# Ten of eleven SwiGLU product blocks turned by VectorE in 32x32 squares and carried by sixteen small DMAs instead of being turned by TensorE

## The chip, the cores and the metric

One core of one Trainium2 chip. The metric is the device time of one execution in microseconds (us). The core has a matrix engine (TensorE, PE in the profile, its weight loads PEld), a vector engine (VectorE, DVE), an activation engine (ScalarE, ACT), GpSimd (POOL), a queue engine (SyncE, SP) and 16 DMA engines that serve the DMA queues of SP, ACT and POOL together.

## What is computed

One layer of a streaming encoder on x of 256 tokens x 2048 channels in fp32: a SwiGLU FFN, a gated mixer (pooling and SSD branches), a cross-attention into 256 memory tokens, and a second FFN. The change touches the two FFNs only:

```python
def swiglu(u, w1, w3, w2):
    return (jax.nn.silu(u @ w1) * (u @ w3)) @ w2

f = swiglu(rms_norm(h, ffn1_pre_g[i]), ffn1_w1[i], ffn1_w3[i], ffn1_w2[i])
h = h + 0.5 * rms_norm(f, ffn1_post_g[i])
```

w1 and w3 are 2048 x 5632, w2 is 5632 x 2048. The product silu(u @ w1) * (u @ w3) comes out with tokens on the partitions, and the multiplication by w2 wants it with the 5632 hidden features on the partitions. Somebody has to transpose it.

## The kernel before

**Tiling.** Every weight matrix is streamed in chunks: 256 rows x 512 columns, 512 KB, laid in SBUF as 128 partitions x 2 x 512. A ring of four slots (`RING`) holds a chunk three times: `raw` as loaded, `wh` its fp32r high part, `wl` the rest. A job is 8 chunks (`CD`) for w1 or w3 and 22 (`CF`) for w2. A chunk of a token-major job is 12 matmuls: 2 halves of the rows, 2 blocks of 128 tokens (`T`), and 3 products each (lines 530 to 532: wh with the low part of the activations, wh with the high part, wl with the high part).

**The four engines of a chunk.** SP loads chunk c into its ring slot when VectorE has split chunk c-4 (semaphore `low`, lines 355 to 360). ScalarE copies `raw` to `wh` (line 879) when the load has landed and TensorE has done chunk c-4 (`used`), so it runs three chunks ahead (`AHEAD`). VectorE then writes `wl = raw - wh` (line 1293). TensorE waits for `high` and `low` of the chunk (lines 509 and 510). ScalarE and VectorE keep their order by hand: `advance()` makes the next split, `to(n)` advances until chunk n is the next of TensorE, and other work is written between such calls.

**An FFN.** It has 11 pairs of jobs (`NP`), one for each block of 512 hidden columns: "gate" (w1, 8 chunks), then "up" (w3, 8 chunks). Pair 0 is written out, pairs 1 to 10 are a loop on each engine. After a gate job ScalarE writes `silu_g` (line 975). After an up job VectorE writes the product `hid` (line 1433), two instructions of 128x512, one for each 128 tokens; their last one also frees the accumulator of the up job.

**The turn.** While the next pair runs, `hid` is transposed. TensorE does it behind the third gate chunk: `turn_hidden` (line 628) waits for `hid` and for the free PSUM area, and `turn` makes 8 transposes of 128x128 (line 565) into that area. ScalarE writes the high part `hidh` from it (`hidden_high`, line 981), VectorE the rest `hidl` (`hidden_low`, line 1421), both behind `to(c0 + 3)`, c0 being the first chunk of the pair. The block of the last pair is turned behind the loop (line 638). Then 4 "down" jobs of 22 chunks multiply `hidh` and `hidl` by w2.

Of the kernel before, what the change touches and what calls it, by code (L numbers as in the profile page):

```python
# [19 lines left out]
ALU = mybir.AluOpType  # L20
# [21 lines left out]
def hybrid_block(nc, x, mem, ffn1_pre_g, ffn1_w1, ffn1_w3, ffn1_w2, ffn1_post_g, mix_pre_g, w_in, b_gate,  # L42
# [74 lines left out]
    def slot(name):  # L117
        return jobs[name][0] % 2

    def moved(name):  # L120

        return jobs[name][0] // 2 + 1
# [8 lines left out]
    areas = {0: [], 1: []}  # L131
    for q in range(4):
        areas[q % 2].append(("pre0", q))
    areas[0] += [("hidden", 0, j) for j in range(NP)]
    for q in range(4):
        areas[q % 2].append(("pre1", q))
    areas[1] += ["dt", "cs", "csT", ("cb", 0), ("cb", 1), ("cb", 2), ("cb", 3)] + [("Y", g) for g in range(GROUPS)]
# [6 lines left out]
    areas[1] += ["score1", "probT1"]  # L144
    for q in range(4):
        areas[q % 2].append(("pre3", q))
    areas[0] += [("hidden", 1, j) for j in range(NP)]

    def use(k, name):

# [10 lines left out]
    with ExitStack() as ctx:  # L161

        def at(name, kb, shape, dt=F32):
            return nc.alloc_sbuf_tensor_at(name, shape, dt, offset=BASE + int(kb * KB))
# [9 lines left out]
        hidl = at("hidl", 140, [P, DFF // P, S], F32R)  # L174
        silu_g = at("silu_g", 184, [P, T, NCOL])
        hid = at("hid", 188, [P, T, NCOL])
        F = at("F", 184, [P, T, D])

        mixh = at("mixh", 96, [P, KD, S], F32R)
# [85 lines left out]
        def sem(name):  # L265
            return ctx.enter_context(nc.semaphore(name))
# [19 lines left out]
        job_squares = sem("job_squares")  # L286
        res_ready = sem("res_ready")
        res_squares = sem("res_squares")
        var_ready = sem("var_ready")
        root_ready = sem("root_ready")  # L290
        normed = sem("normed")
# [37 lines left out]

        def lin(static, i, per):  # L330
            return static if i is None else i * per + static

        def panel(w, k, col):

# [168 lines left out]
        def _(pe):  # L503
# [51 lines left out]
            def claim_area(k, name, i=None, per=1):  # L555
                n = use(k, name) - 1
                if n >= 1:
                    pe.wait_ge(t_moved[k], lin(n, i, per))
# [46 lines left out]
                tr.then_inc(cols_ready, 1)  # L605

            def ffn(f):
                def turn_hidden(j, i=None):

                    pe.wait_ge(evacuated[slot(("up", f, 0))], lin(moved(("up", f, j)), i, 1))  # L610
                    claim_area(0, ("hidden", f, j), i)
                    turn(0, hid)

                def pair(i=None):
                    chunk[0] = first(("gate", f, 0))
                    claim(("gate", f, 0), i)
                    n = {0: 0, 1: 3}[f]
                    if i is None and f == 1:
                        turn_res(n, (0, 1))
                    before = pre_wait(n) if i is None else None  # L620
                    token_chunks(("gate", f, 0), uh, ul, range(0, 2), CD - 1, i, 2 * CD, before)
                    if i is None:
                        turn_res(n, (2, 3))
                        if f == 0:
                            turn_rows()
                    token_chunks(("gate", f, 0), uh, ul, range(2, 3), CD - 1, i, 2 * CD, before)
                    if i is not None:
                        turn_hidden(0, i - 1)
                    token_chunks(("gate", f, 0), uh, ul, range(3, CD), CD - 1, i, 2 * CD, before)
                    if i is None and f == 0:  # L630
                        pe.wait_ge(cols_ready, 4)
                    claim(("up", f, 0), i)
                    token_chunks(("up", f, 0), uh, ul, range(CD), CD - 1, i, 2 * CD)

                pair()
                with pe.Fori(1, NP) as j:
                    pair(j)
                turn_hidden(NP - 1)

                with pe.Fori(0, NJ // 2) as i:  # L640
                    chunk[0] = first(("down", f, 0))
                    for o in range(2):
                        claim(("down", f, o), i)
                        token_chunks(("down", f, o), hidh, hidl, range(CF - 2), CF - 1, i, 2 * CF)
                        pe.wait_ge(t_moved[0], use(0, ("hidden", f, NP - 1)))
                        token_chunks(("down", f, o), hidh, hidl, range(CF - 2, CF), CF - 1, i, 2 * CF)
                chunk[0] = end(("down", f, NJ - 1))
# [217 lines left out]
        def _(act):  # L865
# [99 lines left out]
            def ffn(f):  # L965
                def silu(i=None):
                    done(i, 2 * CD)
                    if i is not None:

                        act.wait_ge(evacuated[slot(("up", f, 0))], lin(moved(("up", f, 0)), i - 1, 1))  # L970
                    if i is None:

                        act.wait_ge(normed, {0: 1, 1: 2 * T + 2}[f])
                    for t in range(T):
                        a = nc.scalar.activation(silu_g[:, t], tok(slot(("gate", f, 0)))[:, t], ACT.Silu, scale=sr_ffn[:, t:t + 1])
                    a.then_inc(evacuated[slot(("gate", f, 0))], 1)

                def hidden_high(i=None, j=0):
                    act.wait_ge(t_ready[0], lin(use(0, ("hidden", f, j)), i, 1))
                    dst = hidh[:, j * M:(j + 1) * M] if i is None else hidh[:, bass.ds(i * M, M)]  # L980
                    nc.scalar.activation(dst, area(0), ACT.Copy).then_inc(t_high[0], 1)

                c0 = first(("gate", f, 0))

                def pair(i=None):
                    if i is not None:
                        at_chunk[0] = c0
                    to(c0 + 3, i, 2 * CD)
                    if i is not None:
                        hidden_high(i - 1)  # L990
                    to(c0 + CD, i, 2 * CD)
                    silu(i)
                    to(c0 + 2 * CD, i, 2 * CD)

                pair()
                with act.Fori(1, NP) as j:
                    pair(j)
                at_chunk[0] = first(("down", f, 0))
                hidden_high(None, NP - 1)
                fetch_root(1 + f)  # L1000
                d0 = first(("down", f, 0))

                if f == 0:
                    with act.Fori(0, NJ // 2) as i:
                        at_chunk[0] = d0
                        for o in range(2):
                            to(d0 + (o + 1) * CF, i, 2 * CF)
                            done(i, 2 * CF)

                            before = names[number(("down", f, o)) - 1]  # L1010
                            act.wait_ge(evacuated[slot(before)], i + moved(before))
# [262 lines left out]
        def _(dve):  # L1274
# [139 lines left out]
            def ffn(f):  # L1414
                c0 = first(("gate", f, 0))
                g, u = ("gate", f, 0), ("up", f, 0)

                def hidden_low(i=None, j=0):
                    dve.wait_ge(t_high[0], lin(high_use(0, ("hidden", f, j)), i, 1))
                    sl = slice(j * M, (j + 1) * M) if i is None else bass.ds(i * M, M)  # L1420
                    nc.vector.tensor_tensor(hidl[:, sl], area(0), hidh[:, sl].bitcast(F32), ALU.subtract).then_inc(t_moved[0], 1)

                def pair(i=None):
                    if i is not None:
                        at_chunk[0] = c0
                    to(c0 + 3, i, 2 * CD)
                    if i is not None:
                        hidden_low(i - 1)
                    to(c0 + 2 * CD, i, 2 * CD)
                    done(i, 2 * CD)  # L1430
                    dve.wait_ge(evacuated[slot(g)], lin(moved(g), i, 1))
                    for t in range(T):
                        h = nc.vector.scalar_tensor_tensor(out=hid[:, t], in0=tok(slot(u))[:, t], scalar=sr_ffn[:, t:t + 1],
                                                           in1=silu_g[:, t], op0=ALU.mult, op1=ALU.mult)
                    h.then_inc(evacuated[slot(u)], 1)

                pair()
                with dve.Fori(1, NP) as j:
                    pair(j)
                at_chunk[0] = first(("down", f, 0))  # L1440
                hidden_low(None, NP - 1)
                d0 = first(("down", f, 0))
                if f == 0:
                    with dve.Fori(0, NJ // 2) as i:
# [399 lines left out]
```

## Time and profile before

| | |
|---|---|
| median of 3 runs | 2801.12 us (2796.75 to 2801.47) |
| profiled execution: span from the first to the last instruction | 2798.7 us |
| TensorE matmuls busy | 2755.3 us, 98% of the span |
| VectorE busy | 1569.6 us, 56% |
| ScalarE busy | 1296.0 us, 46% |
| DMA, mean | 187 GB/s |
| mean granted TensorE clock | 0.994 |

The span leaves out what lies ahead of the first and behind the last instruction; it is 2.4 us below the median of the runs, and inside their spread. A matmul row shows the modelled duration of one matmul, and these overlap: what TensorE needs for a piece of work is read from the distance between the starts of rows, not from the durations. On the rows of a timeline the bracket at the end is the engine's idle time before the row and who ended it. A row "SPq" or "ACTq" is the time that the engine's sequencer took to issue a DMA, not the transfer. A wait of a DMA queue costs nothing as long as the data is there when ScalarE wants it.

### The profile page before, as it was taken

How to read it: one execution, taken by the hardware profiler on the slowest of the kernel's cores; microseconds unless marked ns; L12 is line 12 of the kernel's file. 1: busy time of each engine (PE TensorE's matmuls, PEld its weight loads, DVE VectorE, ACT ScalarE, POOL GpSimd, SP SyncE). 2: the span in 40 equal slices, each digit the busy share in tenths (PEclk: the TensorE clock that was granted, in tenths of full speed). 3: DMA queues.
4: the chain of work that ended last, by engine and by line, in shares of the span. 5: the costliest groups of instructions: out<-in, count | busy, mean ns of one | idle time of the engine just before them, and what ended most of it. 6: DMA issues, size and time to landing. Idle time of an engine off the chain costs nothing.

```text
span 2798.7 us, 39709 instructions
## 1 busy us (share of the span) xinstructions
PE 2755.3 (98%) x14332; PEld 2371.3 (85%) x14332; DVE 1569.6 (56%) x1758; ACT 1296.0 (46%) x1430; POOL 35.3 (1%) x59
## 2 busy tenths in 40 slices
PE   8999999999899999999999999999999999999998
PEld 7888888888799888989999888888978888888886
DVE  5454544444466555787787664556565544454444
ACT  5444444444354444355565554445554444444443
POOL 0000000000000000000000000000000000000000
PEclk9999999999999999999999999999999999999999
DMA  7666666666556666565665675566456666666664
GB/s 224 188 187 193 188 189 190 192 197 196 150 167 195 190 202 188 174 185 176 180 187 179 176 201 189 188 230 191 145 172 188 188 188 193 188 187 194 196 197 150
DMA packets 268277, 522.92 MB, mean 187 GB/s; under 512 B 18496, under 2 KB 18880, under 8 KB 267936
## 3 DMA queue, kind: packets, MB, share of 16 engines
q1 hardware_dynamic: 263104, 504.07, 59.7%
q0 software_dynamic: 5056, 17.68, 2.2%
q8 instruction: 57, 0.93, 0.1%
q14 instruction: 28, 0.23, 0.0%
q10 hardware_dynamic: 32, 0.01, 0.0%
HBM read 519.53 MB, written 2.16 MB: 186 GB/s over the span
## 4 chain that ended last, share of the span: by engine, by line
PE 96%; DVE 2%; DMA 0%; ACT 0%; issue 0%; DVEq 0%; SPq 0%; ACTq 0%
PE J L530 26%; PE J L532 26%; PE J L531 26%; PE J L548 5%; PE J L551 5%; PE J L550 5%; PE A L565 1%; PE A L576 1%; PE A L768 1%; PE A L767 1%; PE A L766 0%; DVE res L1341 0%; DVE wl L1293 0%; DMA raw<-in_w_in_dram 0%; PE A L757 0%
## 5 line engine op out<-in xcount | busy, mean ns | idle before, releaser
L1293 DVE TENSOR_TENSOR wl<-raw,wh 128x1024 fp32r<-128x1024 f32 x950 | 1159.2, 1225 | 1017.3 <-ACT wh L879 1010.2
L879 ACT ACTIVATE wh<-raw 128x1024 fp32r<-128x1024 f32 x950 | 1004.6, 1060 | 1241.9 <-PE J L532 1000.4
L530 PE MATMUL J<-wh,ul 128*128 128x512 f32 x2048 | 804.0, 393 | 5.8 <-DVE bT L1513 2.5
L532 PE MATMUL J<-wl,uh 128*128 128x512 f32 x2048 | 800.4, 391 | 0.0
L531 PE MATMUL J<-wh,uh 128*128 128x512 f32 x2048 | 800.2, 391 | 0.0
L530 PEld LDWEIGHTS J<-wh,ul 128*128 128x128 f32 x2048 | 386.3, 189 | 85.9 <-issue 4.3
L532 PEld LDWEIGHTS J<-wl,uh 128*128 128x128 f32 x2048 | 386.0, 188 | 80.4
L531 PEld LDWEIGHTS J<-wh,uh 128*128 128x128 f32 x2048 | 386.1, 189 | 78.5
L548 PE MATMUL J<-ul,wh 128*128 128x256 f32 x1088 | 310.4, 285 | 1.1 <-DVE wl L1293 1.1
L551 PE MATMUL J<-uh,wl 128*128 128x256 f32 x1088 | 308.4, 284 | 0.0
L550 PE MATMUL J<-uh,wh 128*128 128x256 f32 x1088 | 308.4, 283 | 0.0
L530 PE MATMUL J<-wh,hidl 128*128 128x512 f32 x704 | 274.4, 390 | 0.0
L532 PE MATMUL J<-wl,hidh 128*128 128x512 f32 x704 | 274.3, 390 | 0.0
L531 PE MATMUL J<-wh,hidh 128*128 128x512 f32 x704 | 274.2, 390 | 0.0
L548 PEld LDWEIGHTS J<-ul,wh 128*128 128x128 f32 x1088 | 209.1, 192 | 1.4 <-ACT wh L879 1.3
L550 PEld LDWEIGHTS J<-uh,wh 128*128 128x128 f32 x1088 | 209.1, 192 | 0.0
L551 PEld LDWEIGHTS J<-uh,wl 128*128 128x128 f32 x1088 | 209.0, 192 | 0.0
L531 PEld LDWEIGHTS J<-wh,hidh 128*128 128x128 f32 x704 | 132.2, 188 | 27.3
L530 PEld LDWEIGHTS J<-wh,hidl 128*128 128x128 f32 x704 | 132.2, 188 | 27.3
L532 PEld LDWEIGHTS J<-wl,hidh 128*128 128x128 f32 x704 | 132.2, 188 | 27.3
L530 PE MATMUL J<-wh,ynl 128*128 128x512 f32 x256 | 100.0, 391 | 0.0
L532 PE MATMUL J<-wl,ynh 128*128 128x512 f32 x256 | 99.8, 390 | 0.0
(239 smaller groups left out, 1895.8 us busy)
## 6 DMA issues: line engine op xcount, KB each, us to landing
raw<-in_ffn_w_dram SPq DMA_DIRECT2D x528, 512.0 KB, 4.4
raw<-in_w_in_dram SPq DMA_DIRECT2D x257, 512.0 KB, 3.8
raw<-in_w_ssd_out_dram SPq DMA_DIRECT2D x64, 512.0 KB, 4.1
raw<-in_w_pool_out_dram SPq DMA_DIRECT2D x32, 512.0 KB, 4.2
raw<-in_w_mix_out_dram SPq DMA_DIRECT2D x32, 512.0 KB, 4.5
csb<-cs_dram POOLq DMA_DIRECT2D x16, 512.0 KB, 7.4
raw<-in_pool_w_dram SPq DMA_DIRECT2D x8, 512.0 KB, 4.3
raw<-in_w_k_dram SPq DMA_DIRECT2D x8, 512.0 KB, 4.0
```

The source lines that it names most:

```text
L530: nc.tensor.matmul(o[:, t], b, wh[:, r, kk], start=(k == 0 and kk == 0), stop=False)
L531: nc.tensor.matmul(o[:, t], a, wh[:, r, kk], start=False, stop=False)
L532: mm = nc.tensor.matmul(o[:, t], a, wl[:, r, kk], start=False, stop=(k == last_k and kk == CK - 1))
L548: nc.tensor.matmul(o[:, m], h, b, start=(k == 0 and kk == 0 and m % 2 == 0), stop=False, skip_group_check=True)
L550: nc.tensor.matmul(o[:, m], h, a, start=False, stop=False, skip_group_check=True)
L551: mm = nc.tensor.matmul(o[:, m], l, a, start=False, stop=(k == last_k and kk == CK - 1), skip_group_check=True)
L565: tr = nc.tensor.transpose(o[:, m, t * P:(t + 1) * P], src[:, t, m * P:(m + 1) * P], ident[:])
L576: mm = nc.tensor.matmul(area(q % 2)[:, m, t * P:(t + 1) * P], res[:, t, c], diag[:, t], start=True, stop=True, skip_group_check=True)
L767: nc.tensor.matmul(A[:, 1, 1, c], E[:, h, P:2 * P], Xdt[:, 0, c], start=True, stop=False)
L768: mm = nc.tensor.matmul(A[:, 1, 1, c], E[:, h, 2 * P:3 * P], Xdt[:, 1, c], start=False, stop=True)
L879: nc.scalar.activation(wh[:, r], raw[:, r], ACT.Copy).then_inc(high, 1)
L1293: nc.vector.tensor_tensor(wl[:, r], raw[:, r], wh[:, r].bitcast(F32), ALU.subtract).then_inc(low, 1)
```

## The change

For the blocks of pairs 0 to 9 TensorE makes no transposes. Behind the `hid` of a pair VectorE transposes it in 32x32 squares into a new tile `turned` (`turn_blocks`, two instructions of 128x512, no cross-partition movement beyond 32 partitions). In the next pair ScalarE's queue issues, behind one split, sixteen DMAs (`move_turned`) from `turned` to a new tile `hraw`, each from 32 partitions to 32 partitions with 4 runs of 64 numbers (256 B) per partition: 32 KB each, 512 KB together. `hidh` and `hidl` are made from `hraw` in SBUF by two instructions each instead of one from PSUM, and behind `to(c0 + 6)` instead of `to(c0 + 3)`. The block of pair 10 is still turned by TensorE. Before the down jobs TensorE waits for `hid_low`.

```diff
@@ TensorE
-                    token_chunks(("gate", f, 0), uh, ul, range(2, 3), CD - 1, i, 2 * CD, before)
-                    if i is not None:
-                        turn_hidden(0, i - 1)
-                    token_chunks(("gate", f, 0), uh, ul, range(3, CD), CD - 1, i, 2 * CD, before)
+                    token_chunks(("gate", f, 0), uh, ul, range(2, CD), CD - 1, i, 2 * CD, before)
...
-                turn_hidden(NP - 1)
+                turn_hidden()
+
+                pe.wait_ge(hid_low, turned_before(f + 1))
@@ ScalarE
-                def hidden_high(i=None, j=0):
-                    act.wait_ge(t_ready[0], lin(use(0, ("hidden", f, j)), i, 1))
-                    dst = hidh[:, j * M:(j + 1) * M] if i is None else hidh[:, bass.ds(i * M, M)]
-                    nc.scalar.activation(dst, area(0), ACT.Copy).then_inc(t_high[0], 1)
+                def move_turned(i):
+
+                    act.wait_ge(turned_ready, lin(turned_before(f) + 1, i, 1))
+                    for c in range(M):
+                        for a in range(P // 32):
+                            act.dma_start(hraw[32 * c:32 * (c + 1), :, a * 64:(a + 1) * 64],
+                                          turned[32 * a:32 * (a + 1), c::4].rearrange("p b t n -> p b (t n)")).then_inc(hid_loaded, 16)
+
+                def hidden_high(i):
+                    act.wait_ge(hid_loaded, lin(16 * 16 * (turned_before(f) + 1), i, 16 * 16))
+                    for t in range(T):
+                        a = nc.scalar.activation(in_blocks(hidh[:, bass.ds(i * M, M), t * P:(t + 1) * P]), hraw_blocks(t), ACT.Copy)
+                    a.then_inc(hid_high, 1)
...
-                    to(c0 + 3, i, 2 * CD)
+                    if i is not None:
+                        to(c0 + 1, i, 2 * CD)
+                        move_turned(i - 1)
+                    to(c0 + 6, i, 2 * CD)
                     if i is not None:
                         hidden_high(i - 1)
@@ VectorE
+                def turn_blocks(i=None):
+
+                    dve.wait_ge(evacuated[slot(u)], lin(moved(u), i, 1))
+                    for t in range(T):
+                        tr = nc.vector.transpose(turned[:, :, t], hid[:, t].rearrange("p (b n) -> p b n", n=32))
+                    tr.then_inc(turned_ready, 1)
+
+                def hidden_low(i):
+                    dve.wait_ge(hid_high, lin(turned_before(f) + 1, i, 1))
+                    for t in range(T):
+                        h, l = (in_blocks(x[:, bass.ds(i * M, M), t * P:(t + 1) * P]) for x in (hidh, hidl))
+                        o = nc.vector.tensor_tensor(l, hraw_blocks(t), h.bitcast(F32), ALU.subtract)
+                    o.then_inc(hid_low, 1)
...
-                    to(c0 + 3, i, 2 * CD)
+                    to(c0 + 6, i, 2 * CD)
                     if i is not None:
                         hidden_low(i - 1)
...
                 pair()
-                with dve.Fori(1, NP) as j:
+                turn_blocks()
+                with dve.Fori(1, NP - 1) as j:
                     pair(j)
+                    turn_blocks(j)
+                pair(NP - 1)
```

On ScalarE's queue the head of the loop over the pairs stood like this before; `wh<-raw` is the split of a weight chunk:

```order
L996 ISA
L878 REGISTER_ALU
L879 ACTIVATE wh<-raw 128x1024
L875 REGISTER_ALU
L878 REGISTER_ALU
L879 ACTIVATE wh<-raw 128x1024
L878 REGISTER_ALU
L879 ACTIVATE wh<-raw 128x1024
L979 REGISTER_ALU
L981 ISA
L981 ACTIVATE hidh<-A 128x1024
```

and stands like this now:

```order
L1028 ISA
L894 REGISTER_ALU
L895 ACTIVATE wh<-raw 128x1024
L999 DMA hraw<-turned 32x4x64 x16
L891 REGISTER_ALU
L894 REGISTER_ALU
L895 ACTIVATE wh<-raw 128x1024
L894 REGISTER_ALU
L895 ACTIVATE wh<-raw 128x1024
```

The sixteen DMA issues stand between the first and the second split of a pair; the high part of the product moved behind the sixth split.

On VectorE's queue the end of pair 0 and the head of the loop stood like this before:

```order
L1433 SCALAR_TENSOR_TENSOR hid<-J,stat,silu_g 128x512 x2
L1438 UNCONDITIONAL_BRANCH
L1438 ISA
L1293 TENSOR_TENSOR wl<-raw,wh 128x1024
L1292 REGISTER_ALU
L1293 TENSOR_TENSOR wl<-raw,wh 128x1024
```

and stands like this now:

```order
L1479 SCALAR_TENSOR_TENSOR hid<-J,stat,silu_g 128x512 x2
L1454 STREAM_TRANSPOSE turned<-hid 128x16x32 x2
L1485 UNCONDITIONAL_BRANCH
L1485 ISA
L1325 TENSOR_TENSOR wl<-raw,wh 128x1024
L1324 REGISTER_ALU
L1325 TENSOR_TENSOR wl<-raw,wh 128x1024
```

The two transposes stand behind the product and ahead of the first split of the next pair.

## Rows read from the trace of the kernel before

**Rows 1.** The page: engines' busy time, and the chain that ended last.

```profile
PE 2755.3 (98%) x14332; PEld 2371.3 (85%) x14332; DVE 1569.6 (56%) x1758; ACT 1296.0 (46%) x1430; POOL 35.3 (1%) x59
...
PE 96%; DVE 2%; DMA 0%; ACT 0%; issue 0%; DVEq 0%; SPq 0%; ACTq 0%
```

**Rows 2.** Windows: 44 us of an FFN's pairs; last three columns clock, DMA share, GB/s.

```profile
150.00:194.00 44.00, 44.00 (x200) 36.56 (x199) 21.65 (x20) 18.64 (x20) 0.00 (x0) 1.00 0.66 190
```

**Rows 3.** Timeline around one turn: start us, us, engine, line, operation.

```profile
157.11 0.39 PE L532 MATMUL J<-wl,uh 128*128 128x512 f32 x1
...
157.34 1.03 PE L565 MATMUL A<-ident,hid 128*128 128x128 f32 x8
...
158.13 0.48 PE L530 MATMUL J<-wh,ul 128*128 128x512 f32 x1
...
158.45 0.40 PE L531 MATMUL J<-wh,uh 128*128 128x512 f32 x1
...
158.68 0.39 PE L532 MATMUL J<-wl,uh 128*128 128x512 f32 x1
```

**Rows 4.** Timeline of ScalarE over one pair.

```profile
149.38 1.06 ACT L879 ACTIVATE wh<-raw 128x1024 fp32r<-128x1024 f32 x1 [1.66 <-PE J L532]
152.10 1.06 ACT L879 ACTIVATE wh<-raw 128x1024 fp32r<-128x1024 f32 x1 [1.66 <-PE J L532]
154.82 1.06 ACT L879 ACTIVATE wh<-raw 128x1024 fp32r<-128x1024 f32 x1 [1.66 <-PE J L532]
158.52 1.03 ACT L981 ACTIVATE hidh<-A 128x1024 f32 x1 [2.65 <-PE A L565]
```

**Rows 5.** Timeline at the start of that pair, TensorE's first matmul and VectorE.

```profile
149.18 0.39 PE L530 MATMUL J<-wh,ul 128*128 128x512 f32 x1
...
149.47 1.41 DVE L1433 SCALAR_TENSOR_TENSOR hid<-J,stat,silu_g 128x512 f32<-128x512 f32 x2 [0.49 <-PE J L532]
150.79 1.21 DVE L1293 TENSOR_TENSOR wl<-raw,wh 128x1024 fp32r<-128x1024 f32 x1
```

**Rows 6.** Groups by line: busy us, mean ns of one, idle before and who ended it.

```profile
L1433 DVE SCALAR_TENSOR_TENSOR hid<-J,stat,silu_g 128x512 f32<-128x512 f32 x44 | 31.0, 747 | 10.5 <-PE J L532 10.5
L1641 DVE TENSOR_SCALAR yb<-yb,stat 128x512 f32<-128x512 f32 x16 | 7.1, 484 | 0.3
...
L975 ACT ACTIVATE silu_g<-J,stat 128x512 f32<-128x512 f32 x44 | 27.9, 684 | 34.3 <-PE J L532 34.3
```

**Rows 7.** DMA issues of the queues by line: ns min/median/max, first and last start.

```profile
L360 SPq DMA_DIRECT2D raw<-in_ffn_w_dram x528: 367/373/695, 1.8 to 2768.2; - x176
...
L439 SPq DMA_DIRECT2D out_dram<-res x4: 332/348/366, 2791.8 to 2795.4; - x4
...
L867 ACTq DMA_DIRECT2D rows<-in_ffn_pre_g_dram x1: 430/430/430, 0.9 to 0.9; - x1
```

**Rows 8.** Timeline of SP: issues with no wait between them.

```profile
0.88 0.40 SPq L346 DMA_DIRECT2D ident<-in_identity_dram  x1
1.33 0.43 SPq L372 DMA_DIRECT2D res<-in_x_dram  x1
1.81 0.46 SPq L360 DMA_DIRECT2D raw<-in_ffn_w_dram  x1
...
18.77 0.37 SPq L360 DMA_DIRECT2D raw<-in_ffn_w_dram  x1
19.18 0.47 SPq L377 DMA_DIRECT2D tri<-in_causal_dram  x1
19.69 0.43 SPq L378 DMA_DIRECT2D d_bc<-in_d_skip_dram  x1
```

**Rows 9.** The dt weights, 512 KB in 2048 packets of 256 B: issue, and the DMA then.

```profile
L360 SPq DMA_DIRECT2D raw<-in_w_in_dram x1: 1343/1343/1343, 779.8 to 779.8; - x1
...
DMA to landing us min/median/max: 5.3/5.3/5.3
...
DMA packets 1749, 0.51 MB, mean 255 GB/s; under 512 B 1712, under 2 KB 1712, under 8 KB 1749
```

**Rows 10.** DMAs with KB each and median us to landing, and the range of SP's loads.

```profile
raw<-in_ffn_w_dram SPq DMA_DIRECT2D x528, 512.0 KB, 4.4
csb<-cs_dram POOLq DMA_DIRECT2D x16, 512.0 KB, 7.4
...
DMA to landing us min/median/max: 3.5/4.3/11.0
```

**Rows 11.** Timeline of one split: ScalarE's high part, then VectorE's low part.

```profile
119.46 1.06 ACT L879 ACTIVATE wh<-raw 128x1024 fp32r<-128x1024 f32 x1 [1.66 <-PE J L532]
...
120.55 1.23 DVE L1293 TENSOR_TENSOR wl<-raw,wh 128x1024 fp32r<-128x1024 f32 x1 [1.49 <-ACT wh L879]
```

More of the change, by code:

```diff
@@ L133, in hybrid_block @@
         areas[q % 2].append(("pre0", q))
-    areas[0] += [("hidden", 0, j) for j in range(NP)]
+    areas[0] += [("hidden", 0, NP - 1)]
     for q in range(4):
@@ L146, in hybrid_block @@
         areas[q % 2].append(("pre3", q))
-    areas[0] += [("hidden", 1, j) for j in range(NP)]
+    areas[0] += [("hidden", 1, NP - 1)]
     def use(k, name):
@@ L176, in hybrid_block @@
         hid = at("hid", 188, [P, T, NCOL])
+        turned = at("turned", 192, [P, NCOL // 32, T, 32])
+        hraw = at("hraw", 196, [P, M, S])
         F = at("F", 184, [P, T, D])
@@ L288, in hybrid_block @@
         res_squares = sem("res_squares")
+        turned_ready = sem("turned_ready")
+        hid_loaded = sem("hid_loaded")
+        hid_high = sem("hid_high")
+        hid_low = sem("hid_low")
         var_ready = sem("var_ready")
@@ L331, in lin, with turned_before, in_blocks, hraw_blocks @@
             return static if i is None else i * per + static
+        def turned_before(f):
+            return f * (NP - 1)
+        def in_blocks(x):
+            return x.rearrange("p k (a n) -> p k a n", n=32)
+        def hraw_blocks(t):
+            return hraw[:].rearrange("p k (a t n) -> p k t a n", t=T, n=32)[:, :, t]
         def panel(w, k, col):
@@ L607, in ffn, with turn_hidden @@
             def ffn(f):
-                def turn_hidden(j, i=None):
-                    pe.wait_ge(evacuated[slot(("up", f, 0))], lin(moved(("up", f, j)), i, 1))
-                    claim_area(0, ("hidden", f, j), i)
+                def turn_hidden():
+                    pe.wait_ge(evacuated[slot(("up", f, 0))], moved(("up", f, NP - 1)))
+                    claim_area(0, ("hidden", f, NP - 1))
                     turn(0, hid)
@@ L976, in silu, with last_high @@
                     a.then_inc(evacuated[slot(("gate", f, 0))], 1)
-                def hidden_high(i=None, j=0):
-                    act.wait_ge(t_ready[0], lin(use(0, ("hidden", f, j)), i, 1))
-                    dst = hidh[:, j * M:(j + 1) * M] if i is None else hidh[:, bass.ds(i * M, M)]
-                    nc.scalar.activation(dst, area(0), ACT.Copy).then_inc(t_high[0], 1)
+                def move_turned(i):
[9 more added lines that the diff above has]
+                    a.then_inc(hid_high, 1)
+                def last_high():
+                    act.wait_ge(t_ready[0], use(0, ("hidden", f, NP - 1)))
+                    nc.scalar.activation(hidh[:, (NP - 1) * M:NP * M], area(0), ACT.Copy).then_inc(t_high[0], 1)
                 c0 = first(("gate", f, 0))
@@ L998, in ffn @@
                 at_chunk[0] = first(("down", f, 0))
-                hidden_high(None, NP - 1)
+                last_high()
                 fetch_root(1 + f)
@@ L1416, in ffn, with last_low @@
                 g, u = ("gate", f, 0), ("up", f, 0)
-                def hidden_low(i=None, j=0):
-                    dve.wait_ge(t_high[0], lin(high_use(0, ("hidden", f, j)), i, 1))
-                    sl = slice(j * M, (j + 1) * M) if i is None else bass.ds(i * M, M)
+                def turn_blocks(i=None):
[9 more added lines that the diff above has]
+                    o.then_inc(hid_low, 1)
+                def last_low():
+                    dve.wait_ge(t_high[0], high_use(0, ("hidden", f, NP - 1)))
+                    sl = slice((NP - 1) * M, NP * M)
                     nc.vector.tensor_tensor(hidl[:, sl], area(0), hidh[:, sl].bitcast(F32), ALU.subtract).then_inc(t_moved[0], 1)
@@ L1437, in ffn @@
                 pair()
-                with dve.Fori(1, NP) as j:
+                turn_blocks()
+                with dve.Fori(1, NP - 1) as j:
                     pair(j)
+                    turn_blocks(j)
+                pair(NP - 1)
                 at_chunk[0] = first(("down", f, 0))
-                hidden_low(None, NP - 1)
+                last_low()
                 d0 = first(("down", f, 0))
```

## The prediction

> **What bounds the kernel now.** I read the page first: TensorE is busy 98% of the span, and the chain that ended last lies to 96% on it [rows 1]. The next question is whether it is short of anything in the pairs of the FFNs, where the change is. The window of 44 us there shows TensorE busy for all 44.00 us at full clock, VectorE for 21.65 and ScalarE for 18.64, the DMA engines two thirds busy at 190 GB/s [rows 2]. So in a pair the time is the number of matmuls and nothing else, and work taken from TensorE is time gained, as long as the other engines still deliver each chunk by its turn. The timeline shows how close that is. ScalarE starts a split every 2.72 us (149.38, 152.10, 154.82) and has idled 1.66 us before each, waiting for TensorE [rows 4]; 2.72 us is the pace of a chunk. It runs three chunks ahead, so it can be late by some chunks once, but not without limit.
>
> **What is removed.** The turn: the 8 transposes start at 157.34, the next matmul at 158.13, 0.79 us later, and the one behind that 0.32 us later (158.45) where 0.23 is usual (158.68) [rows 3]. That is 0.79 + 0.09 = 0.88 us. It happens in 10 pairs of 2 FFNs: 20 x 0.88 = **17.6 us**, all on TensorE's path. The PSUM area's handoffs (ScalarE's 1.03 us from PSUM [rows 4]) go from a place where nobody waits for them to another such place.
>
> **What is added, on VectorE.** Two transposes per pair, 128x512 in fp32, SBUF to SBUF. The trace has none. An instruction of that size with one input from SBUF takes 484 ns, the one with two inputs, one of them in PSUM, 747 ns [rows 6]; I take 0.6 us, nearer to the one-input row, so 1.2 us for two (ends: 1.0 and 1.5). The first split of the pair on VectorE is that much later, and it has almost three chunks of room, so by itself this costs nothing; it counts only as the start of what follows. The two-part `hidl` costs some 0.2 us more than before in VectorE's idle half: nothing.
>
> **What is added, on ScalarE's queue.** This is the term that decides. Let S be the first matmul of a pair, 149.18 in the trace [rows 5]. VectorE begins the product at S + 0.29 and has both halves at S + 1.70 (149.47 + 1.41 = 150.88) [rows 5]. With 0.05 for the semaphore and 1.2 for the transposes, `turned` is there at S + 2.95, and ScalarE, which has made one split (149.38 to 150.44, [rows 4]), passes its wait at about S + 3.0. Then its sequencer issues 16 DMAs, and behind them, on the same in-order queue, stands the split of the pair's fifth chunk (the second split of the pair; before, it started at 152.10 = S + 2.92). That split takes 1.06 us, VectorE starts 0.03 later and takes 1.23 [rows 11]; with 0.05 to reach TensorE this is 2.37 us. TensorE wants this chunk after four chunks, at S + 4 x 2.72 = S + 10.88 (without the turn). So the 16 issues are hidden if they take no more than 10.88 - 3.0 - 2.37 = 5.5 us, 0.344 us each. **Each 0.01 us more of an issue costs 0.16 us of stall per pair, 3.2 us in all.**
>
> What does an issue take? SP's lone issues of a 512 KB load take 367 to 373 ns, the output's 332 to 366; ScalarE's only one took 430 ns at the start [rows 7]. Between issues with no wait between them lie about 0.05 us more, and the issues themselves are then longer: start to start 0.45 and 0.48 us at the start of the program, 0.41 and 0.51 at 18.77 to 19.69 us, when nothing else starts up, the last being 128 runs of 256 B as each of the new DMAs is [rows 8]. The single DMA of 2048 runs took 1.34 us to issue [rows 9]: against the 0.37 for 256 runs this is 0.54 ns per run, which by a straight line gives 0.30 for 128 runs. So the ends are 0.30 + 0.05 = 0.35 and 0.51 us. I take **0.46 us**, the mean of the two distances from 18.77 to 19.69, since only these rows show what the new code does, issue behind issue. Then 16 x 0.46 = 7.36 us, the split starts at S + 10.4, the chunk is complete at S + 12.75, and TensorE stalls 12.75 - 10.88 = 1.87 us. Behind it ScalarE and VectorE need 1.06 and 1.23 us for each chunk of 2.72, so they catch up and the next chunk is in time. One stall per pair: 20 x 1.87 = 37.4 us.
>
> **The DMAs.** 512 KB more per pair of 43.5 us, beside 8 MB of weights: 6% more bytes. In 2 us of the dt load 1749 packets, 1712 of them small, were moved at 255 GB/s [rows 9], so all 2048 packets of a pair are worth some 2.4 us of the 16 engines if they come at once; spread over 7.4 us of issues they take a third of them, and a third of the engines is idle [rows 2]. During the issues few loads are in flight, because SP waits for the late split. The load of the ninth chunk is held back by the fifth's low part, to S + 12.7; it lands in 4.4 us [rows 10] at S + 17.1, needs 2.3 us more, and is due at S + 12.75 + 10.88 = S + 23.6. That leaves 4 us. The high part of `hid` is wanted only behind the down jobs; ScalarE reaches its wait at about S + 18, 7 us behind the last issue. Cost: nothing.
>
> A rule that speaks against the change: TensorE's 8 transposes cost 0.88 us, 0.11 us each [rows 3]. The Trainium skill, "VectorE: DVE Perf Modes", section "The three transpose paths", gives 311 ns for a 128x128 by VectorE in 32x32 blocks only, and under "Rules for kernel authors" advises TensorE for 128x128 if PSUM is acceptable. The nearest row, 484 ns for four such widths in one instruction, says less than half of that per block [rows 6]. By the page's figure, taken for each of 8 blocks, an estimate is 2.5 us instead of 1.2, and the sum would be 26 us more than mine.
>
> **The sum.** -17.6 + 37.4 = +19.8 us. The profiled span of 2798.7 us becomes 2818.5; against the median of the runs, 2801.1, which is 2.4 us above the span, it is **2821 us**, 0.7% slower.
>
> **The rivals.**
>
> *The issues are about as short as the lone ones.* At 0.376 to 0.411 us from start to start the stall is 0.5 to 1.1 us per pair and gives back what the turn saved, within 5.6 us. A lone output issue and a gap, 0.348 + 0.045, lies right there [rows 7, 8]. Time: 2801.
>
> *The burst is hidden, the change does what it says.* At 0.344 us or less from start to start (the straight line's 0.30 + 0.05 reaches that) TensorE never waits, and all 17.6 us are gained: 2783.5. Against it: no row of one issue behind another is below 0.41 us [rows 8]. Between 0.344 and 0.376 part of the gain is left.
>
> *The transfers are late.* The ninth chunk's load or the 2048 small packets delay each other. The point from which this counts: that load may take 23.6 - 2.3 - 12.7 = 8.6 us to land. Usually it takes 4.4, GpSimd's 512 KB transfers take 7.4, and the longest load of SP took 11.0 [rows 10]. At 11.0 the second stall is 2.4 us, 20 x 2.4 = 48 us on top: 2869. For it: the landing of a transfer in many small packets beside loads; against it: 255 GB/s with such packets [rows 9]. The Trainium skill, "DMA: Bandwidth & Descriptors", section "Bandwidth", calls transfers under 64 KB descriptor-dominated, which points to this rival; the rows on the 256 B packets don't bear it out, and no row shows sixteen transfers of 32 KB.
>
> **How the numbers follow.** The forecast, issues of 0.42 to 0.52 us: 0.50. Even: 0.17. Gain, in part or in full: 0.20, the full one 0.10 of it. Late transfers, or transposes and issues beyond my ends: 0.13. So faster 0.20, same 0.17, slower 0.63; "same" is within 0.2%, 5.6 us, about what a measurement of this kernel can tell from no change. The upper bounds of both terms together, 0.51 us per issue and 1.5 us of transposes, give a stall of 2.97 us and +41.8 us: 2843. The range of 8 in 10 goes a little over that to 2850, which takes in a mild form of late transfers, and down to 2788, which takes in the partial gains and leaves out the full one.
>
> **What the profile of the changed kernel would show.** In a pair, sixteen issues on ScalarE's queue with starts 0.46 us apart; the split behind them near S + 10.4; a wait of TensorE for VectorE's low part of the fifth chunk, 20 times about 1.9 us; the transposes at 0.6 us; no wait of ScalarE for `hraw`; SP's loads landing as before. TensorE idle nowhere else in the pairs. The prediction is wrong if the starts are below 0.41 us apart, if the transposes take above 0.9 us each, or if TensorE waits at the ninth chunk too.

## The result and the profile after

The changed kernel takes 2937.78 us (median of 4 runs, 2937.66 to 2939.8) against 2800.39 us before (4 runs): ratio 1.0492, interval 1.0479 to 1.0504. It is 137 us slower, where 20 us had been forecast; the time lies outside the range of 2788 to 2850. The span of the profiled execution grew from 2798.7 to 2936.2 us, 137.5 us or **6.88 us for each of the 20 pairs** with the new path.

The page of the kernel after, engines and chain, for [rows 1]:

```profile
span 2936.2 us, 39777 instructions
...
PE 2791.8 (95%) x14172; PEld 2388.2 (81%) x14172; DVE 1591.8 (54%) x1818; ACT 1291.5 (44%) x1450; POOL 35.3 (1%) x59
...
PE 86%; ACTq 7%; DVE 4%; issue 1%; ACT 1%; DMA 0%; DVEq 0%; SPq 0%
```

There are 160 matmuls fewer, and yet TensorE's busy time rose by 36.5 us. Of the chain that ended last 7% is now ScalarE's queue; before it was nothing. The waits of TensorE show one new line (engine, line, who was waited for, us in total, times, longest):

```profile
PE J L548 <- DVE wl L1325: 101.5, 21, 5.1
```

Before it was 1.1 us, once, at the start. One pair of the kernel after, on ScalarE and VectorE (timeline: start us, us, engine), for [rows 4, 5]; the pair's first matmul starts at 163.72:

```profile
163.93 1.06 ACT L895 ACTIVATE wh<-raw 128x1024 fp32r<-128x1024 f32 x1 [1.66 <-PE J L550]
166.79 10.40 ACTq L999 DMA_DIRECT2D hraw<-turned  x16
177.38 3.90 ACT L895 ACTIVATE wh<-raw 128x1024 fp32r<-128x1024 f32 x4 [12.39 <-issue]
...
164.01 1.41 DVE L1479 SCALAR_TENSOR_TENSOR hid<-J,stat,silu_g 128x512 f32<-128x512 f32 x2 [0.49 <-PE J L550]
165.46 1.30 DVE L1454 STREAM_TRANSPOSE turned<-hid 128x512 f32<-128x512 f32 x2
166.69 1.18 DVE L1325 TENSOR_TENSOR wl<-raw,wh 128x1024 fp32r<-128x1024 f32 x1
178.47 4.63 DVE L1325 TENSOR_TENSOR wl<-raw,wh 128x1024 fp32r<-128x1024 f32 x4 [10.60 <-ACT wh L895]
```

The burst of sixteen issues lasts 10.40 us, and the split behind it starts at 177.38, 13.66 us into the pair. And TensorE in that pair, its first matmul and the place of the stall, for [rows 3]:

```profile
163.72 0.39 PE L548 MATMUL J<-wh,ul 128*128 128x512 f32 x1
...
174.38 0.39 PE L550 MATMUL J<-wl,uh 128*128 128x512 f32 x1
179.84 0.76 PE L548 MATMUL J<-wh,ul 128*128 128x512 f32 x1 [5.07 <-DVE wl L1325]
180.40 0.63 PE L549 MATMUL J<-wh,uh 128*128 128x512 f32 x1
180.82 0.63 PE L550 MATMUL J<-wl,uh 128*128 128x512 f32 x1
...
184.24 0.63 PE L549 MATMUL J<-wh,uh 128*128 128x512 f32 x1
184.66 0.51 PE L550 MATMUL J<-wl,uh 128*128 128x512 f32 x1
185.01 0.40 PE L548 MATMUL J<-wh,ul 128*128 128x512 f32 x1
185.25 0.39 PE L549 MATMUL J<-wh,uh 128*128 128x512 f32 x1
```

Two losses stand here. The next matmul was due 0.23 us after 174.38 and starts 5.46 us after it: 5.23 us of stall. Then the matmuls start 0.43 us apart instead of 0.23, until 184.66: the 12 matmuls of the chunk take 5.17 us (179.84 to 185.01) where 2.72 is usual, 2.45 us more. The windows around it name the reason (columns as in [rows 2], the third from the right is the granted clock):

```profile
170.00:174.60 4.60, 4.60 (x22) 3.60 (x20) 0.00 (x0) 0.00 (x0) 0.00 (x0) 1.00 0.50 143
174.60:179.70 5.10, 0.17 (x1) 0.00 (x0) 1.23 (x2) 2.32 (x3) 0.00 (x0) 0.84 0.19 38
...
182.00:184.00 2.00, 2.00 (x6) 1.52 (x6) 1.10 (x1) 0.00 (x0) 0.00 (x0) 0.50 1.05 402
...
186.00:190.00 4.00, 4.00 (x19) 3.31 (x18) 3.44 (x4) 2.38 (x4) 0.00 (x0) 1.00 0.54 172
```

The mean of 0.84 in the window of the stall says that the granted clock fell while TensorE still waited. After the stall TensorE runs at clock 0.50, the lower of its two levels (1.2 GHz), and returns to 1.00 some 5 us later. The sum closes: -0.88 + 5.23 + 2.45 = 6.80 us per pair, 136 us for 20, and 137.5 are measured.

### The profile page after: what moved, and what is told of

Read it like the earlier page. It is cut to its first block, busy times and chain, and to the rows that moved or that the text cites. A ratio compares the mean times of both kernels' runs of the same rounds, so it can differ in the third digit from the quotient of the medians.

```text
span 2936.2 us, 39777 instructions
## 1 busy us (share of the span) xinstructions
PE 2791.8 (95%) x14172; PEld 2388.2 (81%) x14172; DVE 1591.8 (54%) x1818; ACT 1291.5 (44%) x1450; POOL 35.3 (1%) x59
## 4 chain that ended last, share of the span: by engine, by line
PE 86%; ACTq 7%; DVE 4%; issue 1%; ACT 1%; DMA 0%; DVEq 0%; SPq 0%
PE J L548 23%; PE J L549 23%; PE J L550 23%; ACTq L999 7%; PE J L566 5%; PE J L568 5%; PE J L569 5%; DVE wl L1325 1%; DVE hid L1479 1%; ACT wh L895 1%; PE A L583 1%; PE A L594 1%; DVE turned L1454 1%; PE A L784 0%; PE A L783 0%
## 5 line engine op out<-in xcount | busy, mean ns | idle before, releaser
L548 PE MATMUL J<-wh,ul 128*128 128x512 f32 x2048 | 823.6, 402 | 106.7 <-DVE wl L1325 101.5
L549 PE MATMUL J<-wh,uh 128*128 128x512 f32 x2048 | 818.6, 400 | 0.0
L550 PE MATMUL J<-wl,uh 128*128 128x512 f32 x2048 | 816.6, 399 | 0.0
L548 PEld LDWEIGHTS J<-wh,ul 128*128 128x128 f32 x2048 | 399.2, 195 | 199.6 <-ACT wh L895 110.0
L550 PEld LDWEIGHTS J<-wl,uh 128*128 128x128 f32 x2048 | 397.2, 194 | 85.5
L549 PEld LDWEIGHTS J<-wh,uh 128*128 128x128 f32 x2048 | 397.6, 194 | 82.5
```

What stands on the lines that cost most here:

```text
L548: nc.tensor.matmul(o[:, t], b, wh[:, r, kk], start=(k == 0 and kk == 0), stop=False)
L549: nc.tensor.matmul(o[:, t], a, wh[:, r, kk], start=False, stop=False)
L550: mm = nc.tensor.matmul(o[:, t], a, wl[:, r, kk], start=False, stop=(k == last_k and kk == CK - 1))
```

## Experiments

Two theories stood after this. **A**: everything lost is the late split, because sixteen issues stand ahead of it on ScalarE's queue, plus the clock that falls behind the stall; the way over VectorE and the DMAs costs nothing in itself. **B**: the transfers or transposes cost too. And two questions: why an issue takes 0.62 us, where the kinds of issue in [rows 7] took 0.35 to 0.43 us in the median, and how the clock depends on the stall.

### Taking the burst apart

**Eight and eight.** The second half of the issues moves behind the fourth split:

```diff
-                        to(c0 + 1, i, 2 * CD)
-                        move_turned(i - 1)
+                        to(c0 + 1, i, 2 * CD)
+                        move_turned(i - 1, range(0, 8))
+                        to(c0 + 4, i, 2 * CD)
+                        move_turned(i - 1, range(8, 16))
```

> Eight issues behind the first split, eight behind the fourth. With issues 0.65 us from start to start the first burst takes 5.2 us, and by the prediction's own sum (10.88 - 3.1 - 2.37 = 5.4 us) this is just hidden. If the late split is the whole loss: no stall above 0.1 us per pair, full clock, 2783 us. If it is above 2790, something else of the burst costs too.

Measured: 2783.33 us (one run; before on that chip 2800.35), clock 0.995. In the window from 150 to 500 us, in which eight such bursts stand, TensorE waits for no split at all. The first burst lasts 5.16 us and is hidden, as the prediction's own bound of 5.4 to 5.5 us said. So the whole loss hangs on the length of the burst in front of that one split; the same sixteen transfers, transposes and issues are still there.

**Two behind each of eight splits**, the high and low parts at `to(c0 + 11)` on both engines:

```diff
-                        to(c0 + 1, i, 2 * CD)
-                        move_turned(i - 1)
+                        to(c0 + 1, i, 2 * CD)
+                        move_turned(i - 1, range(0, 2))
+                        to(c0 + 2, i, 2 * CD)
+                        move_turned(i - 1, range(2, 4))
...
+                        to(c0 + 8, i, 2 * CD)
+                        move_turned(i - 1, range(14, 16))
```

> The changed kernel with the sixteen issues laid out two behind each of eight splits of ScalarE, and the high and low parts of the product behind the eleventh split instead of the sixth. Nothing else moves. Theory A (the burst in front of one split is the whole loss): 2 x 0.65 + 1.06 + 0.2 = 2.56 us of ScalarE per chunk of 2.72 us, no stall of TensorE in the pairs, clock 0.99, and the full 17.6 us of the turn gained: ratio to before 0.994, some 2783 us. Theory B (the transfers themselves, or VectorE's transposes, cost something that the burst hides): above 0.998.

Measured: 2783.22 us against 2801.38, ratio 0.9935 (0.9918 to 0.9951), clock 0.994. Theory A holds, and B, which wanted a ratio above 0.998, doesn't: the full gain of the removed turns is there, 16.6 us of span. Its timeline of ScalarE shows something more:

```profile
157.21 1.06 ACT L895 ACTIVATE wh<-raw 128x1024 fp32r<-128x1024 f32 x1 [1.41 <-PE J L550]
157.22 1.25 ACTq L1002 DMA_DIRECT2D hraw<-turned  x2
159.93 1.06 ACT L895 ACTIVATE wh<-raw 128x1024 fp32r<-128x1024 f32 x1 [1.66 <-PE J L550]
159.94 1.25 ACTq L1002 DMA_DIRECT2D hraw<-turned  x2
```

The two issues behind a split run beside it: they begin 0.01 us after the activation, not after its end. The expected sum of 2.56 us per chunk counted both one after the other; here two issues delay nothing. The kernel with eight and eight shows more. Its second eight stand behind the fourth split of the pair:

```profile
157.43 1.06 ACT L895 ACTIVATE wh<-raw 128x1024 fp32r<-128x1024 f32 x1 [7.16 <-PE J L550]
157.66 1.25 ACTq L1002 DMA_DIRECT2D hraw<-turned  x2
158.40 1.05 ACT L895 ACTIVATE wh<-raw 128x1024 fp32r<-128x1024 f32 x1
...
159.35 1.04 ACT L895 ACTIVATE wh<-raw 128x1024 fp32r<-128x1024 f32 x1
```

They begin at 157.66, when only the second split has started; the third and fourth, ahead of them in the code, start at 158.40 and 159.35. So the issues delayed the split that stood behind them, and did not wait for the ones ahead of them to run.

### Another queue

**GpSimd's queue** issues the sixteen, in a straight row of code with constants to wait on; ScalarE's queue has no DMA:

```diff
-                        to(c0 + 1, i, 2 * CD)
-                        move_turned(i - 1)
...
+            def carry(f, i):
+                pool.wait_ge(turned_ready, turned_before(f) + i + 1)
+                for c in range(M):
+                    for a in range(P // 32):
+                        pool.dma_start(hraw[32 * c:32 * (c + 1), :, a * 64:(a + 1) * 64],
+                                      turned[32 * a:32 * (a + 1), c::4].rearrange("p b t n -> p b (t n)")).then_inc(hid_loaded, 16)
...
+                for i in range(NP - 1):
+                    carry(f, i)
```

> The same sixteen DMAs issued from GpSimd's queue, which is idle there; ScalarE's queue holds splits and activations only. Theory A (the issues cost because of the queue they stand in): no stall of TensorE, full clock, ratio 0.994, some 2783 us, whatever an issue costs on GpSimd (16 x 0.5 to 0.9 us = 8 to 14 us, done before ScalarE wants hraw at about 15.5 us into the pair, or a short wait of it that its three chunks of lead take up). Theory B (small transfers beside the loads delay these): SP's loads land above 4.4 us and TensorE waits.

Measured: 2781.83 us, ratio 0.9929 (0.9912 to 0.9945), clock 0.995. An issue takes 0.549 us there, the sixteen 8.65 us, and ScalarE waits 1.3 us per pair for the data (26.4 us in all), which delays nobody: TensorE waits for no split. SP's loads land in 4.3 us. It is 0.7% below the kernel before, and no kernel here that computes the whole layer was faster. The Trainium skill, "Trainium Kernel Development and Optimization", section "Key Constraints", says that issuing from several queues "only saves the sequencer's issue time"; here that time, with the stall and the lower clock that came of it, was all there was to save, and it was 156 us of 2938.

**SP's queue** issues the burst, ahead of the load of the pair's eighth chunk; `carry` issues them as on GpSimd's queue:

```diff
...
+                    def carry_here(k, j=j):
+                        if k == 7:
+                            carry(f, j - 1)
-                    load_job(w1[0], bass.ds(j * NCOL, NCOL), CD, j, 2 * CD)
+                    load_job(w1[0], bass.ds(j * NCOL, NCOL), CD, j, 2 * CD, carry_here)
```

> The same burst of sixteen issues, on SP's queue, ahead of the load of the pair's eighth chunk. It asks whether an issue is dear because ScalarE issues it or because of the transfer's form. Theory A1 (ScalarE's sequencer is slower than SP's): issues of about 0.37 us, 6.6 us for the sixteen, that load goes out at S + 9.8 us and lands in time, ratio 0.994. Theory A2 (the form, or issue behind issue, costs, whoever issues): 0.62 us each, 10.4 us for sixteen, the load goes out at S + 13.5 and lands at S + 17.9, chunk complete at S + 20.2 where it is due at S + 19.0: a stall of 1.2 us per pair, and 24 us in all against 17.6 gained.

Measured: 2810.33 us (one run). The two kinds of issue on one queue (ns min/median/max), this kernel's, and the loads of the kernel after:

```profile
L390 SPq DMA_DIRECT2D hraw<-turned x320: 585/601/744, 65.5 to 2523.4; - x160
...
L378 SPq DMA_DIRECT2D raw<-in_ffn_w_dram x528: 367/373/661, 1.8 to 2905.7; - x176
```

A2 holds: 0.60 us also on SP. It isn't ScalarE's sequencer. The burst lasts 10.30 us, the load goes out late, and TensorE waits 19.5 us in all, 1.1 of them at the start of the program.

### Why an issue takes 0.62 us

**One run of 1 KB per partition** in place of four of 256 B, both tiles laid out for it:

```diff
-        turned = at("turned", 192, [P, NCOL // 32, T, 32])
-        hraw = at("hraw", 196, [P, M, S])
+        turned = at("turned", 192, [P, M, NCOL // P, T, 32])
+        hraw = at("hraw", 196, [P, P // 32, M, T, 32])
...
```

> The changed kernel with both tiles laid out so that each of the sixteen DMAs moves one run of 1 KB per partition instead of four of 256 B: 32 runs per DMA instead of 128. Same bytes, same place in the queue. Theory F1 (an issue costs by its runs): well below 0.62 us, 0.4 or less, stall under 1.5 us per pair, some 2810 us. Theory F2 (fixed price of an issue between SBUF tiles of 32 partitions): 0.6 us again, stall 5 us, some 2937 us.

**Four DMAs of 128 partitions**, with four runs each and with one. Both kernels leave out the crossing of partitions, so their product block is wrong; they show what the issues cost. The edit for four runs:

```diff
-                        for a in range(P // 32):
-                            act.dma_start(hraw[32 * c:32 * (c + 1), :, a * 64:(a + 1) * 64],
-                                          turned[32 * a:32 * (a + 1), c::4].rearrange("p b t n -> p b (t n)")).then_inc(hid_loaded, 16)
+                        act.dma_start(hraw[:, :, c * 64:(c + 1) * 64],
+                                      turned[:, c::4].rearrange("p b t n -> p b (t n)")).then_inc(hid_loaded, 16)
...
```

> Four DMAs of 128 partitions x 4 runs of 256 B in place of sixteen of 32 partitions, same bytes and same number of runs in all. They leave out the crossing of partitions, so the product block is wrong; only the cost of the issues and the transfer is looked at. Theory F1 (by runs): 512 runs per issue, each above 0.8 us. Theory F3 (by partitions or engines, few partitions being the dear case): about 0.37 us, as SP's loads. Theory F2 (fixed): 0.6 us. In all three the four issues take under 5.2 us, so no stall and the full gain: 2783 us.

> As wide4, four DMAs of 128 partitions, but one run of 1 KB per partition; the crossing of partitions is again left out. With the changed kernel, run1 and wide4 this makes a table of two by two, partitions by runs. F1: the cheapest of the four, under 0.4 us. F2: 0.6 us. F3: as wide4. Time 2783 us by all.

Measured, the median of an issue on ScalarE's queue:

| | runs per partition: 4 | runs per partition: 1 | time, us (one run) |
|---|---|---|---|
| 32 partitions, 16 issues per pair | 622 ns | 612 ns | 2937.78 (median of 4) and 2936.81 |
| 128 partitions, 4 issues per pair | 672 ns | 622 ns | 2781.22 and 2781.85 |

Between 32 runs per DMA and 512 lie 60 ns. F2 holds: the price is nearly fixed, and neither runs nor partitions make it. Sixteen issues cost 3.7 to 3.9 times what four do for the same bytes.

**Through device memory.** One store behind the first split, four loads behind the third; the layout of the one-run kernel:

```diff
...
+                    act.dma_start(hid_dram, turned[:].rearrange("p c b t n -> p c (b t n)")).then_inc(hid_stored, 16)
+
+                def fetch_turned(i):
+
+                    act.wait_ge(hid_stored, lin(16 * (turned_before(f) + 1), i, 16))
+                    for c in range(M):
+                        act.dma_start(hraw[32 * c:32 * (c + 1)].rearrange("p a k t n -> p a (k t n)"),
+                                      hid_dram[:, c].rearrange("(a p) n -> p a n", p=32)).then_inc(hid_loaded, 16)
...
```

> The crossing of partitions goes through device memory: behind the first split of a pair ScalarE's queue issues one store of 512 KB from `turned`, behind the third split four loads of 128 KB, each of 32 partitions x 4 runs of 1 KB, into `hraw`. Theory G (an issue is dear, 0.6 us, where both sides are SBUF, and costs 0.37 us where one side is device memory, as SP's loads do): store and loads issue in 0.35 to 0.4 us. Theory H (0.6 us is what an issue costs on this queue or next to this work): 0.6 us here too. By both the five issues are hidden and the time is 2783 us, ratio 0.994; 1 MB more of memory traffic per pair of 43.5 us makes SP's loads land later than 4.4 us by some tenths.

Measured: 2781.83 us, ratio 0.9932 (0.9915 to 0.9949). The issues of the three kinds on ScalarE's queue, this kernel's two and the changed kernel's:

```profile
L999 ACTq DMA_DIRECT2D hid_dram<-turned x20: 344/345/352, 63.3 to 2488.4; - x20
...
L1005 ACTq DMA_DIRECT2D hraw<-hid_dram x80: 309/453/512, 66.6 to 2492.7; - x80
...
L999 ACTq DMA_DIRECT2D hraw<-turned x320: 592/622/727, 64.1 to 2644.4; - x160
```

G holds in its main point: with device memory on one side an issue takes 0.345 us for the store and 0.453 for the loads, which stand one behind the other, range up to 0.512 and lie above the 0.35 to 0.4 expected; with SBUF on both sides no form was below 0.61 in the median on this queue. SP's loads land in 4.4 us as before in spite of the added traffic. Why two SBUF sides cost more isn't known; no run opens that.

### Stall and clock

Twelve or eleven issues in the burst, the others behind the fifth split, give stalls of other lengths. The edit for twelve; the other has 11 in place of 12:

```diff
-                        move_turned(i - 1)
+                        move_turned(i - 1, range(0, 12))
+                        to(c0 + 5, i, 2 * CD)
+                        move_turned(i - 1, range(12, 16))
```

> The changed kernel with twelve issues in the burst and four more behind the fifth split of the pair. By 16 issues = 10.4 us and a stall of 5.2 us, four issues fewer take 2.6 us from both: stall 2.6 us per pair. It asks what of the loss is clock. Theory C1 (the clock falls behind any stall of some us): behind the stall 11 matmuls at 0.43 us instead of 0.23, some 2.4 us per pair more, in all 20 x (2.6 + 2.4 - 0.88) = +82 us. Theory C2 (this stall is too short to lower it): 20 x (2.6 - 0.88) = +34 us, all matmuls at 0.23 us from start to start.

> Eleven issues in the burst, five behind the fifth split: by the runs so far a stall of 5.23 - 5 x 0.65 = 2.0 us per pair. With a stall of about 1.3 us the granted clock stayed at full, with 2.6 us it fell behind the stall. If the clock stays: 20 x (2.0 - 0.88) = +22 us, 2823. If it falls as behind 2.6 us: 20 x 1.8 us more, 2859.

Measured: 2870.39 and 2827.85 us (one run each). TensorE behind the stall, with twelve:

```profile
170.99 0.47 PE L548 MATMUL J<-wh,ul 128*128 128x512 f32 x1 [2.44 <-DVE wl L1330]
171.30 0.40 PE L549 MATMUL J<-wh,uh 128*128 128x512 f32 x1
...
172.36 0.63 PE L550 MATMUL J<-wl,uh 128*128 128x512 f32 x1
172.78 0.63 PE L548 MATMUL J<-wh,ul 128*128 128x512 f32 x1
...
174.92 0.63 PE L550 MATMUL J<-wl,uh 128*128 128x512 f32 x1
175.34 0.45 PE L548 MATMUL J<-wh,ul 128*128 128x512 f32 x1
```

Two stalls of the kernel with eleven:

```profile
165.83 0.47 PE L548 MATMUL J<-wh,ul 128*128 128x512 f32 x1 [1.79 <-DVE wl L1330]
166.14 0.40 PE L549 MATMUL J<-wh,uh 128*128 128x512 f32 x1
...
168.22 0.39 PE L549 MATMUL J<-wh,uh 128*128 128x512 f32 x1
...
256.99 0.47 PE L548 MATMUL J<-wh,ul 128*128 128x512 f32 x1 [1.79 <-DVE wl L1330]
...
258.45 0.60 PE L548 MATMUL J<-wh,ul 128*128 128x512 f32 x1
258.84 0.63 PE L549 MATMUL J<-wh,uh 128*128 128x512 f32 x1
259.27 0.63 PE L550 MATMUL J<-wl,uh 128*128 128x512 f32 x1
...
261.83 0.43 PE L550 MATMUL J<-wl,uh 128*128 128x512 f32 x1
```

Behind the first the matmuls keep their distance of 0.23 us. Behind the second, which is as long, they are 0.43 us apart from 258.84 to 261.83. The trace has this behind 2 of the 20 stalls with eleven, and behind all 20 with twelve. Of the theories on twelve C1 holds in kind, with eight slow matmuls where eleven were expected: +69 us for +82.

Four lengths of the idle time, all behind issues of these transfers. The idle time per pair is the wait's total, less the 1.1 us of the start, over 20; the rest is what the span grew per pair, plus the 0.88 us gained, less the idle time:

| kernel | idle per pair, us | growth of the span per pair | rest | stalls of 20 with a fall of the clock | clock of the whole span |
|---|---|---|---|---|---|
| burst on SP | 0.92 | +0.50 | 0.46 | 0 | 0.994 |
| eleven in the burst | 1.76 | +1.38 | 0.50 | 2 | 0.993 |
| twelve | 2.42 | +3.50 | 1.96 | 20 | 0.983 |
| sixteen, the change | 5.02 | +6.88 | 2.74 | 20 | 0.971 |

In every rest stand 0.16 us because the wait is counted from the modelled end of the last matmul, that much after the next was due, and some 0.1 because the first two matmuls behind it start 0.31 instead of 0.23 us apart. A fall of the clock costs 1.6 us with eleven or twelve in the burst and some 2.4 us with sixteen, read from the starts of the matmuls behind the stall. That leaves at most 0.2 us per pair, 4 us of span; the spans of the kernel before differ by more, from 2794.3 to 2802.9 us. A single issue more in the burst, the twelfth, made 2828 into 2870 us: 0.65 us of it per pair is the issue, 1.5 the clock, which now falls each time. The Trainium skill, "TensorE: Matmul & The Clock Gate", section "Why this matters for your kernels", advises against idle gaps between bursts of matmuls for that reason; the traces agree, and here the clock fell behind every idle time of 2.4 us in a kernel that is otherwise 100% busy there. Why it fell behind two idle times of 1.8 us and not behind eighteen like them stays open.

## Why the prediction was wrong, step by step

**What bounds the kernel, and what the turn is worth.** Right. Four ways of hiding or moving the issues give 2781.8 to 2783.3 us, 16 to 19 us of span below the kernel before, against the 17.6 worked out from 0.88 us per turn.

**The mechanism and its place.** Right: the split behind the burst is late, TensorE waits for the low part of the pair's fifth chunk, once per pair. The start of the burst was put at S + 3.0 us, and it is at S + 3.07 (166.79 - 163.72). The transposes take 690 ns each against 600 taken:

```profile
L1454 DVE STREAM_TRANSPOSE turned<-hid 128x512 f32<-128x512 f32 x40 | 26.1, 690 | 0.7
```

The estimate from the 311 ns that the Trainium skill, "VectorE: DVE Perf Modes", section "The three transpose paths", gives for a 128x128 in bf16, 1.24 us for each instruction, was too high by a factor of almost two: a block of 128x128 within such an instruction takes 172 ns in fp32.

**The failed step: 0.46 us for an issue.** The price was taken from two distances between issues of SP (0.41 and 0.51 us), and 0.51 was called the upper end. (The issue of 128 runs of 256 B that the prediction named with it took 0.43 us itself; the 0.51 us is the distance behind the issue ahead of it.) Measured are 0.65 us from start to start, 10.40 us for the sixteen instead of 7.36. All rows that served as a bound, lone or not, had device memory on one side [rows 7, 8]; the trace of before held no DMA from SBUF to SBUF, and the prediction called one of them equal to the new ones because it had as many runs of the same size. The runs show that runs and partitions hardly count and the two SBUF sides do. That the issues stand one behind the other was the lesser resemblance: the loads from device memory that did so took 0.45 us. Why two SBUF sides cost more stays open. The forecast fell short by 117 us, and this step explains 3.04 x 20 = 61 of them; another 0.3 us per pair of the stall, 6 us, are the transposes, the 0.19 us between the last issue and the split, and the last handoff. With the measured stall in place of 1.87 us the prediction's sum would have been -17.6 + 20 x 5.23 = +87 us, 2888.

**The missed step: what a stall does to the clock.** The sum counted a stall at its own length. Behind 5.2 us of stall come 2.45 us of half clock, 49 us in all, a third of the loss. At the forecast stall of 1.87 us (some 1.7 idle) it would have been nearly right to leave it out, as the kernel with eleven shows: 2 falls, some 3 us in all. So the two errors are tied: the wrong price of the issue also hid the second term. The trace of before shows the same thing between the first FFN and the mixer, where TensorE had been idle for 9.70 us: the granted clock of the window from 758 to 768 us is 0.71. The prediction didn't weigh it. The row of TensorE's timeline, and the window:

```profile
756.57 2.04 PE L576 MATMUL A<-diag,res 128*128 128x128 f32 x8 [9.70 <-DVE diag L1385]
...
758.00:768.00 10.00, 9.44 (x59) 9.15 (x59) 4.08 (x12) 3.34 (x9) 0.00 (x0) 0.71 0.01 2
```

**The rivals.** "The burst is hidden" and "the issues are short" failed with the price. "The transfers are late" failed too: the loads land in 4.3 us and the small transfers in 1.9. In the kernel with the issues spread, where both meet, the small ones land in 3.6 us and the loads in 4.5, and nothing waits. The prediction's own test, wrong "if the starts are below 0.41 us apart", looked to the wrong side. Issues beyond its ends had, together with late transfers and slow transposes, a chance of 0.13, and the range up to 2850 left them out. The band of the first rival (issues as short as the lone ones), 0.376 to 0.411 us, was worked out with 5.4 us of room; with the 5.5 us of the prediction's sum it would be 0.382 to 0.417, which changes nothing here.

## What to carry to other kernels

A queue that issues DMAs between other work has a budget: work out when the first instruction behind the issues must start, and divide. Here it was 5.5 us for sixteen issues of 0.65, and splitting them eight and eight, or giving them to the idle GpSimd queue, turned 4.9% slower into 0.6 to 0.7% faster with the same work. If the trace has no row with the same two sides of a transfer, the nearest rows don't bound its issue from above; leave the upper end open, and ask at which stall TensorE's clock would start to fall, since from there a stall can be paid about one and a half times, as here (5.23 + 2.45 us for 5.23).

## What the runs showed of the hardware

- An issue of a DMA with SBUF on both sides takes 0.61 to 0.67 us in the median on ScalarE's queue, whether of 32 or 128 partitions and of 32 to 512 runs, and for 32 partitions and 128 runs 0.60 on SP's and 0.549 on GpSimd's. With device memory on one side the kinds of issue read here took 0.35 to 0.45 us in the median on ScalarE's and SP's queues; only the single one of 2048 runs took 1.34.
- Issues on ScalarE's queue behind an activation that they don't depend on run beside it: two issues of 1.25 us together began 0.01 us after the activation of 1.06 us did. Others began before two activations ahead of them in the code had started (157.66 against 158.40 and 159.35).
- TensorE's clock stayed full behind all 20 idle times of 0.7 to 1.2 us; it fell to half behind 2 of 20 of 1.7 to 1.8 us and behind all 20 of 2.4 us, for about 3 us of matmuls each; with 5 us idle it fell during the stall and stayed low for about 5 us of matmuls.
- 32 KB from SBUF to SBUF in 128 runs of 256 B landed in 1.9 us in the burst, where few loads were in flight, and in 3.6 us between loads; these landed in 4.3 and 4.5 us against 4.4 before.
